# A key's and queries' rotary partner by transfers inside SBUF instead of products with constant matrices

## The reference, cut to what matters

```
q = rmsnorm(q.reshape(B, S, 8, 64), g_q);  k = rmsnorm(k.reshape(B, S, 2, 64), g_k)
q = apply_axial_rope(q, cos, sin);         k = apply_axial_rope(k, cos, sin)

def rotate_half(a):
    a1, a2 = jnp.split(a, 2, axis=-1)
    return jnp.concatenate([-a2, a1], axis=-1)

def apply_axial_rope(x, cos, sin):
    xr, xc = jnp.split(x, 2, axis=-1)
    rot = jnp.concatenate([rotate_half(xr), rotate_half(xc)], axis=-1)
    return x * cos + rot * sin
```

## Time and profile before

| | us |
|---|---|
| median of 3 runs | 750.63 |
| lowest and highest | 750.09, 750.79 |
| span of the profiled execution, first to last instruction | 747.1 |
| TensorE busy in it | 731.6 |
| VectorE busy | 585.6 |
| ScalarE busy | 467.6 |
| GpSimd busy | 147.4 |

### The profile page before, as it was taken

One profiled execution on the slowest core, in us unless ns is written; L12 is line 12 of the kernel. 1 busy time (PEld: TensorE's weight loads), 2 busy tenths in 40 slices (PEclk: granted clock), 3 DMA queues, 4 the chain that ended last, 5 costly groups with the idle time before them and its releaser, 6 DMA issues.

```text
span 747.1 us, 14444 instructions
## 1 busy us (share of the span) xinstructions
PE 731.6 (98%) x5355; PEld 670.1 (90%) x5355; DVE 585.6 (78%) x868; ACT 467.6 (63%) x789; POOL 147.4 (20%) x141
## 2 busy tenths in 40 slices
PE   8999999999999999999999999999999999999996
PEld 7899999888999798998889888997889999999995
DVE  7997989844976577786686998988789888866667
ACT  7878775659765475455554539668686555555565
POOL 5000000001234024333232330010003212343330
PEclk9999999999999999999999999999999999999999
DMA  8554444155555849889787882953237775566551
GB/s 303 162 179 148 157 135 130 48 140 186 173 180 177 309 148 405 302 299 329 240 267 275 265 323 78 347 189 99 82 109 228 259 236 187 183 193 192 179 170 57
DMA packets 47314, 150.68 MB, mean 202 GB/s; under 512 B 9472, under 2 KB 10888, under 8 KB 47256
## 3 DMA queue, kind: packets, MB, share of 16 engines
q1 hardware_dynamic: 45272, 145.86, 58.3%
q10 hardware_dynamic: 1984, 4.03, 1.6%
HBM read 147.73 MB, written 1.06 MB: 199 GB/s over the span
## 4 chain that ended last, share of the span: by engine, by line
PE 80%; DVE 9%; ACT 4%; issue 2%; SPq 2%; DMA 2%; ACTq 0%; DVEq 0%
PE ps L823 29%; PE ps L764 19%; PE ps L511 17%; DVE wl L1767 2%; PE ps L1066 2%; SPq L409 1%; ACT wh L1181 1%; PE ps L1126 1%; PE ps L618 1%; PE ps L1007 1%; DMA ada_w<-in_w_ada 1%; PE ps L637 1%; PE ps L525 1%; PE ps L529 1%; PE ps L526 1%
## 5 line engine op out<-in xcount | busy, mean ns | idle before, releaser
L1767 DVE TENSOR_TENSOR wl<-raw,wh 128x1024 fp32r<-128x1024 f32 x220 | 283.6, 1295 | 88.2 <-ACT wh L1181 86.6
L1181 ACT ACTIVATE wh<-raw 128x1024 fp32r<-128x1024 f32 x220 | 231.5, 1055 | 70.2 <-PE ps L764 46.5
L823 PE MATMUL ps<-xh,wh 128*128 128x256 f32 x672 | 189.7, 282 | 0.5 <-ACT zv L1630 0.5
L823 PE MATMUL ps<-xh,wl 128*128 128x256 f32 x672 | 188.2, 280 | 0.0
L823 PE MATMUL ps<-xl,wh 128*128 128x256 f32 x672 | 188.1, 280 | 0.0
L823 PEld LDWEIGHTS ps<-xh,wh 128*128 128x128 f32 x672 | 126.5, 188 | 4.9 <-issue 2.1
L823 PEld LDWEIGHTS ps<-xl,wh 128*128 128x128 f32 x672 | 126.5, 188 | 1.9
L823 PEld LDWEIGHTS ps<-xh,wl 128*128 128x128 f32 x672 | 126.7, 189 | 0.0
L511 PE MATMUL ps<-xh,wh 128*128 128x256 f32 (+2 forms) x400 | 116.8, 292 | 1.3 <-DVE wl L1767 0.6
L511 PE MATMUL ps<-xh,wl 128*128 128x256 f32 (+2 forms) x400 | 113.2, 283 | 0.0
L511 PE MATMUL ps<-xl,wh 128*128 128x256 f32 (+2 forms) x400 | 113.1, 283 | 0.0
(11 more groups left out here) (420 smaller groups left out, 1238.0 us busy)
## 6 DMA issues: line engine op xcount, KB each, us to landing
raw<-in_w_stream SPq DMA_DIRECT2D x220, 512.0 KB, 4.1
ada_w<-in_w_ada SPq DMA_DIRECT2D x48, 512.0 KB, 6.3
vtk<-in_x SPq DMA_DIRECT2D x2, 512.0 KB, 4.7
tg_m<-in_ln_rows ACTq DMA_DIRECT2D x2, 512.0 KB, 6.7
out<-ob SPq DMA_DIRECT2D x4, 256.0 KB, 2.0
u<-uT SPq DMA_DIRECT2D x16, 34.0 KB, 2.6
eepp<-in_s_mats SPq DMA_DIRECT2D x1, 512.0 KB
decay_rows<-decay_dram SPq DMA_DIRECT2D x4, 128.0 KB
```

The costliest lines, as they stand in the source:

```text
L823: mm = nc.tensor.matmul(ps[:, bank, 0:SEQ], w, x, start=(k == 0), stop=(k == 3 * KD - 1))
L1181: nc.scalar.activation(wh[:, b % RING], raw[:, b % RING], ACT.Identity).then_inc(hi_done, 1)
L1767: V.tensor_tensor(wl[:, b % RING], raw[:, b % RING], wh[:, b % RING].bitcast(F32), ALU.subtract).then_inc(lo_done, 1)
```

## The change

The head dimensions of q and k are put in another order by the host (columns of the weights, the gains): 0 to 15, 32 to 47, 16 to 31, 48 to 63. The partner of a dimension then lies 32 partitions away, for both axes at once, and the sign goes into the sine table. In place of `turn_pairs`, ScalarE's queue issues four DMAs for each tile that exchange neighbouring groups of 32 partitions of `qg` into `qrot` (now with two buffers). In place of `swap_k` it issues two DMAs that exchange the halves of the finished key. VectorE multiplies the fetched partner in SBUF by the sine. The constant matrices go, bank 3 keeps v alone, and VectorE's `q_finish(2)` moves behind `maxima(1)`.

```diff
-            def turn_pairs(t):
-
-                bank3(lambda: nc.tensor.matmul(ps[:, 3, 0:SEQ], cst[:, C_ROT:C_ROT + P], qg[:, t % 3, :], start=True, stop=True))
 
             def k_stat():
 
                 pe.wait_ge(S["q_ev"], 1)
                 nc.tensor.matmul(ps[:, 2, 0:SEQ], cst[:, C_BLK:C_BLK + P], qs[:, 0, :], start=True, stop=True).then_inc(S["q_stat"], 1)
-                turn_pairs(0)
...
-                turn_pairs(i + 1)
-
-            def swap_k():
-
-                pe.wait_ge(S["qk_ready"], 1)
-                bank3(lambda: nc.tensor.matmul(ps[:, 3, 0:SEQ], cst[:, C_SWAP:C_SWAP + P], kf[:, 0, :], start=True, stop=True))
...
                 pe.wait_ge(S["qk_ready"], 2 + i)
                 if i == 0:
-                    pe.wait_ge(S["b3_free"], 4)
+                    pe.wait_ge(S["respread"], 544)
                     pe.wait_ge(S["tok_pre"], QT)
...
                 if n == 12:
-                    swap_k()
                     tok_ms()
...
+            def fetch_partner(t):
+
+                act.wait_ge(S["q_ev"], t + 1)
+                if t >= 2:
+                    act.wait_ge(S["qk_ready"], t - 1)
+                for a in range(0, P, HD // 2):
+                    z = a + HD // 2 if a % HD == 0 else a - HD // 2
+                    act.dma_start(qrot[z:z + HD // 2, t % 2, :], qg[a:a + HD // 2, t % 3, :]).then_inc(partner(t)[0], 16)
+
+            def swap_k():
+
+                act.wait_ge(S["qk_ready"], 1)
+                for n in range(2):
+                    act.dma_start(kf[HD * (1 - n):HD * (2 - n), 1, :], kf[HD * n:HD * (n + 1), 0, :]).then_inc(S["respread"], 16)
+
...
                     if t >= 3:
                         act.wait_ge(S["qk_ready"], t - 2)
                         act.wait_ge(S["q_stat"], t - 2)
-                        act.wait_ge(S["b3_full"], ROTATED[t - 3])
                     nc.scalar.activation(qs[:, t % 3, :], p_, ACT.Square)
                     nc.scalar.activation(qg[:, t % 3, :], p_, ACT.Identity, scale=col("g_q" if t else "g_k"))\
                         .then_inc(S["q_ev"], 1)
+                    fetch_partner(t)
+                    if t == 2:
+                        swap_k()
...
             def q_finish(t):
 
                 dst = qf[:, t - 1, :] if t else kf[:, 0, :]
-                dve.wait_ge(S["b3_full"], reads[0] + 1)
+                dve.wait_ge(S["q_ev"], t + 1)
                 if t == 0:
                     dve.wait_ge(S["mixing_landed"], 48)
-                bank3_read(V.tensor_tensor(qrot[:, :], ps[:, 3, 0:SEQ], rope[:, 1, :], ALU.mult))
                 step(V.tensor_tensor(dst, qg[:, t % 3, :], rope[:, 0, :], ALU.mult))
-                dve.wait_ge(S["b3_free"], reads[0])
-                ins = V.tensor_tensor(dst, dst, qrot[:, :], ALU.add)
+                dve.wait_ge(*partner(t))
+                step(V.tensor_tensor(qrot[:, t % 2, :], qrot[:, t % 2, :], rope[:, 1, :], ALU.mult))
+                ins = V.tensor_tensor(dst, dst, qrot[:, t % 2, :], ALU.add)
...
                 if n == 12:
                     q_finish(1)
-                    dve.wait_ge(S["b3_full"], reads[0] + 1)
-                    bank3_read(V.tensor_copy(kf[:, 1, :], ps[:, 3, 0:SEQ]))
                 if n == 13:
-                    q_finish(2)
                     q_scales(0)
                     maxima(0)
                     maxima(1)
+                    q_finish(2)
                 lo(B_IN2 + n + AHEAD)
```

More of the change, by code:

```diff
@@ L87 @@
 NGATE = 32 + HEADS
-C_ID, C_ONE, C_BLK, C_ROT, C_SWAP, C_MASK, C_T = 0, 128, 256, 384, 512, 640, 768
+C_ID, C_ONE, C_BLK, C_MASK, C_T = 0, 128, 256, 384, 512
 C_ONE_ = C_T + NCK
@@ L265, in two_blocks @@
         qstd = sb("qstd", [P, 2, SEQ])
-        qrot = sb("qrot", [P, SEQ])
+        qrot = sb("qrot", [P, 2, SEQ])
         qf = sb("qf", [P, QT, SEQ])
@@ L314, in two_blocks @@
             "z_act", "zv_turned", "zv_copied", "zv_ms", "zv_std", "zv_n", "mixed", "tok_pre", "tok_done", "tok_sq", "tok_pairs", "tok_sum",
-            "q_ev", "q_stat", "q_std", "b3_full", "b3_free", "v2_ev", "qk_ready",
+            "q_ev", "q_stat", "q_std", "even_partner", "odd_partner", "v2_ev", "qk_ready",
             "s_done", "max_done", "exp_done", "pt_done", "pt_copied", "o_done", "ao_done", "ao_turned",
@@ L364, in lo_made, with partner @@
             return lo_done, t + b + 1
+        def partner(t):
+            return S["odd_partner" if t % 2 else "even_partner"], 64 * (t // 2 + 1)
         def turned_at(tag, m):
@@ L905, in mix_tokens @@
                 mm.then_inc(S["mixed"], 1)
[L907 to L914, removed]
             def turn_v2():
@@ L919, in turn_v2 @@
                 pe.wait_ge(S["zv_copied"], NT)
[L921 to L925, removed]
-            def turn_pairs(t):
-                bank3(lambda: nc.tensor.matmul(ps[:, 3, 0:SEQ], cst[:, C_ROT:C_ROT + P], qg[:, t % 3, :], start=True, stop=True))
+                for c in range(NT):
+                    mm = nc.tensor.transpose(ps[:, 3, c * P:(c + 1) * P], vv[:, c * P:(c + 1) * P], ident)
+                mm.then_inc(S["zv_turned"], 1)
             def k_stat():
@@ L996, in weigh_v @@
                 if i == 0:
+                    pe.wait_ge(S["zv_n"], NT + 1)
                     pe.wait_ge(S["q_std"], 3)
                     pe.wait_ge(S["branch_std"], NT)
-                elif i == 1:
-                    pe.wait_ge(S["b3_free"], 7)
-                else:
+                elif i >= 2:
                     pe.wait_ge(S["branch_lo"], QT + i - 1)
@@ L2370, in _ @@
                     dve.wait_ge(S["mixing_landed"], 48)
-                    dve.wait_ge(S["b3_full"], reads[0] + 1)
-                    bank3_read(V.tensor_copy(vtok[:, :, :].rearrange("p s e -> p (s e)"), ps[:, 3, 0:SEQ]))
+                    dve.wait_ge(S["zv_turned"], NT + 1)
+                    V.tensor_copy(vtok[:, :, :].rearrange("p s e -> p (s e)"), ps[:, 3, 0:SEQ]).then_inc(S["zv_n"], 1)
                     for m in range(QT):
@@ L2655 @@
     up2, down2 = _tiles(w2), I["w_down_2"][0].reshape(KF2, P, D)
-    t2 = _tiles(w1)
+    pairs = np.concatenate([np.arange(0, 16), np.arange(32, 48), np.arange(16, 32), np.arange(48, 64)])
+    heads = np.arange(5 * P).reshape(-1, HD)[:, pairs].reshape(-1)
+    t2 = _tiles(np.concatenate([w1[:, heads], w1[:, 5 * P:]], 1))
     att, tok = I["w_out_2"][0].reshape(2, D // 2, D)
@@ L2692 @@
         "b_ada": _cols(I["b_ada_2"][0].reshape(NMOD, D)[list(MOD_ORDER)].reshape(-1)), "g_norm1": _cols(I["g_norm1_2"][0]),
-        "g_q": twice(I["g_q_2"][0]), "g_k": twice(I["g_k_2"][0]), "g_tok_v": twice(I["g_tok_v_2"][0]),
+        "g_q": twice(I["g_q_2"][0][pairs]), "g_k": twice(I["g_k_2"][0][pairs]), "g_tok_v": twice(I["g_tok_v_2"][0]),
         "g_attn": _cols(I["g_attn_out_2"][0]), "g_tok": _cols(I["g_tok_out_2"][0]), "g_norm2": _cols(I["g_norm2_2"][0]),
@@ L2708 @@
         consts[64 * g:64 * g + 64, C_BLK + 64 * g:C_BLK + 64 * g + 64] = 1.0 / HD
-    for o in range(P):
-        a = o % 32
-        src, sign = (o + 16, -1.0) if a < 16 else (o - 16, 1.0)
-        consts[src, C_ROT + o] = sign
-        consts[(o + 64) % P, C_SWAP + o] = 1.0
     consts[:, C_MASK:C_MASK + P] = np.where(np.arange(P)[:, None] <= np.arange(P)[None, :], 0.0, -1e30)
@@ L2719 @@
     ar, ac = ((n // 64).astype(f)[:, None] * inv, (n % 64).astype(f)[:, None] * inv)
-    ang = np.concatenate([ar, ar, ac, ac], 1).T
-    rope = np.stack([np.concatenate([np.cos(ang)] * 2), np.concatenate([np.sin(ang)] * 2)], 1).astype(f)
+    ang = np.concatenate([ar, ac], 1).T
+    rope = np.stack([np.concatenate([np.cos(ang)] * 4), np.concatenate([-np.sin(ang), np.sin(ang)] * 2)], 1).astype(f)
     arrays = {
```

6 lines of the change are left out of this document (removed).

## The result

| | before | after |
|---|---|---|
| median, us | 750.65 | 760.17 |
| lowest and highest, us | 750.09, 750.79 (4 runs) | 758.60, 761.45 (4 runs) |
| span of the profiled execution, us | 747.1 | 756.8 |
| TensorE busy in it, us | 731.6 | 731.4 |

The change makes the kernel slower: the ratio is 1.0132, with a 95% interval of 1.0119 to 1.0144. The forecast was 756.0 us and its range ended at 759.6, so the sign was right and the size was not. The profile after is that of the fastest of the four executions (758.60 us); the medians are compared, and the profile is read for where the time goes.

What follows compares the result with a forecast made beforehand. TensorE was taken as the bound, with ScalarE and VectorE equally late at two points. Its 2.6 us saved go into waiting, and ScalarE's issues make the stage 5.4 us late: 750.6 + 5.4 = 756.0 us, range 750.1 to 759.6.

Steps and rivals of the forecast that it cites:

- What is added on ScalarE: 22 DMA issues in ScalarE's instruction stream, 0.38 us each from start to start, delaying everything of ScalarE's behind them.
- 760 at 0.63: Forecast time in us if each issue takes 0.63 us, with ScalarE's fourth fetch overtaking VectorE by 0.6 us.
- dear issues: Rival: issues cost 0.60 us, as transfers inside SBUF on SyncE; 760 us, range 757.5 to 761, chance 0.12.
- Step 1: After tile 1's evacuation: four issues put the weights' high part at 496.8, key ready at 500.45 instead of 498.98.
- Step 2: Tile 2's fetches and the swap: six issues, 2.3 us, over at 502.8; scores of pair 0 stand until 504.7.
- Step 3: Query statistics' root at 508.7, first exponentials at 510.6, scores of pair 1 at 513.3, 4.3 us late.
- Step 4: VectorE's maxima and rotations set the exponentials of heads 2 and 3 at 517.1, 5.4 us late.
- Step 5: From those exponentials through the weighting of v to the kernel's end, everything simply starts 5.4 us late.
- Cheap issues: Rival: issues cost ScalarE next to nothing and VectorE sets the stage's end; 750.2 us, no change, chance 0.13.
- The clock: Rival: TensorE's clock falls in its stands, 4.0 us at 509.3 being the border; 757.5 to 759.5 us, chance 0.10.
- Faster: Rival: fetches end before holding anyone, so TensorE's 2.6 us come through; 748.0 us, chance 0.09.
- Late landing: Rival: transfers land late, ahead of scores of pair 0; up to 3 us beyond 2.2 stays hidden, changing nothing.

Runs made afterwards that it cites:

- prices: Kernel after plus eight groups of four DMA issues on ScalarE's queue behind the last store; issues with both ends in SBUF took 0.51 to 0.62 us each.
- sp_swap_early: Against sp_queue, the key's swap is issued one weight block earlier in SyncE's order; 750.05 us, ratio 1.0004 to the kernel before.
- keep_clock: Kernel after with 28 idle constant products on TensorE ahead of the scores of pair 0; 758.95 us, ratio 1.0127 to before.
- sp_maxima_first: Against sp_swap_early, VectorE's rotation of pair 2 moved behind the maxima of heads 2 and 3; 748.18 us, ratio 0.9978 to before.
- swap_first: Kernel after with the two swap issues ahead of the third fetch, all still on ScalarE's queue; 759.27 us, ratio 1.0129 to before.
- sp_queue: Kernel after with all 22 transfers on SyncE's queue and the swap ahead of the fetch for tile 2; 753.45 us, ratio 1.0051 to before.
- hbm_source: Kernel after with every fetch and swap reading a constant HBM table instead of the SBUF tiles; 757.16 us, ratio 1.0104 to before.

## Why the prediction was right and wrong

**The step that failed is the term "What is added on ScalarE"**, the price of an issue: 0.38 us taken, with 0.33 and 0.63 as ends; 0.61 measured, some 0.64 from start to start. The row of the transfer inside SBUF, 0.60, was on the table and was called the nearest in bytes and partitions; it was then put aside because its pattern has more dimensions. The plain rectangles took 0.61 all the same, and the prices run shows that with both ends in SBUF neither bytes nor rows count. At 0.25 more for each of 14 issues in a row that is 3.5 us, and the prediction's own line for it, "760 at 0.63", is what came: 760.17. The profile agrees: its span is 9.7 us longer, where that line makes it 9.5. That the median hits the line within 0.2 us is partly luck. The prediction carried over the 3.5 us between span and median as fixed; in the profiled execution of the kernel after 1.8 us lie outside the span, and the median is 1.6 above that execution for a reason that wasn't seen. The chance of 0.12 on dear issues was too small, and the range ended 0.6 us under the measured time, though the text had priced this case at up to 761.

**Step 1** (high part at 496.8, key ready at 500.45): 497.94 and 501.7. The fetch adds 2.68 us between evacuation and high part (3.04, from 494.90 to 497.94, against 0.36) instead of 1.67.

**Step 2** (six issues over at 502.8, scores of pair 0 at 504.7): 505.6 and 507.99. The six issues took 3.8 us instead of 2.3, on top of the late key. What I left out of the prediction is TensorE's stand of 1.70 us at 499.50: `q_stat(0)` waits for ScalarE's root of the key. It cost nothing of its own, since TensorE would have stood that much longer ahead of the scores.

**Step 3** (root 508.7, first exponentials 510.6, scores of pair 1 at 513.3): 512.54, 514.40 and 517.12, so 3.8 us beyond, of which 3.5 are the price and 0.17 the stage's later start. That the exponentials wait for ScalarE's own stream and no longer for VectorE's maxima is as said: the 0.94 us of idling ahead of them is gone.

**Step 4** (517.1 for the exponentials of heads 2 and 3, by VectorE): 521.42, by ScalarE. VectorE's 7.7 us from its first maximum were right (513.26 + 7.7 = 520.96), and the fourth fetch overtakes it by 0.46 us, where the text had 0.6 for a price of 0.63.

**Step 5** (one constant shift from there): right in form. 9.74 us at the exponentials, 9.87 at the weighting of v, 9.7 in the span. "The 2.6 us taken from TensorE are spent in waiting" is right too, and sp_swap_early shows that they would have been spent so even with free issues.

**The rivals.** Cheap issues: refuted at once, no issue was under 0.51. The Trainium skill (SBUF — State Buffer, "The DMA setup-cost knee") gives the setup two parts, some 50 ns of the sequencer and a few hundred ns of descriptor generation; the prediction took only the first for what ScalarE loses. The 0.61 us measured here is nearer to both together. As a thought experiment the case was well priced: with the issues off ScalarE's stream sp_swap_early came out at 1.0004, where the text had 750.2, and its exponentials of head 2 are 0.34 us early, where the text had 0.4. Dear issues: this is what happened. The clock: it did fall, to 0.50 within the stand of 4.18 us. The Trainium skill (TensorE: Matmul & The Clock Gate, "What's actually happening") says that the slow state is the default and that activity lifts it; the trace agrees, with 0.50 from 506 on, after TensorE's last matmul at 503.8. The prediction's border at a stand of 4 us does not hold: the clock fell 2.2 us into this one, and stands of 2.53 and 2.54 us went either way (last section). keep_clock shows that the fall lay beneath ScalarE's delay and did not add to it. Faster: the gain exists, and it took a queue that nobody waits behind, an earlier swap and a new order on VectorE. That its 748.0 was near the 748.18 of sp_maxima_first is luck, since the path was another: it is VectorE's order behind the exponentials of pair 0 and not their start that decided. Late landing: the swap took 3.1 us to land instead of 2.2, and swap_first and keep_clock move the scores of pair 0 by -3.2 and +2.4 us with the stage within 0.2 us of that of the kernel after, so this slack is real while ScalarE is as late as there. In sp_queue it is gone, and the landing is what is left.

## What to carry to other kernels

Count what a DMA issue costs the engine that issues it, by a row of the trace whose two ends lie in the same kinds of memory, and put the issues on a queue behind which nothing urgent stands; then look at what that queue itself waits for ahead of them. Work taken from the busiest engine pays only up to the next engine's order: where two engines arrive at a point within a few tenths of a microsecond, the order of the second may have to be changed with it; here each of the two edits alone measured as nothing.

## What the runs showed of the hardware

An issue with both ends in SBUF held the engine for 0.61 us, on ScalarE (kernel after, prices) as on SyncE (sp_queue: a group of four in 2.44 to 2.52 us), and on ScalarE for 8 KB as for 128 KB. In prices 32 rows from HBM took 0.44 and a row to HBM 0.27; other shapes with an end in HBM took 0.33 to 0.61. Single issues took longer: 1.47 us in the first fetch of the kernel after (a group of four in 3.40 us instead of 2.44), 1.93 in hbm_source; why is open. Twenty-eight small constant products in two passes took 6.50 us, 0.12 for a pass, so such filling must be counted in full where something waits behind it.

The length of a stand alone did not decide over TensorE's clock. In keep_clock it stayed at 2.4 GHz through a stand of 2.54 us (scores of pair 1, 1.13 us long), in hbm_source it fell to 1.2 GHz within one of 2.53:

```profile
523.39 2.08 PE L956 MATMUL ps<-kf,qf 64*128 64x256 f32 x8 [2.53 <-DVE qf L2302]
```

In swap_first it fell 1.4 us after TensorE had taken up work again behind a stand of only 0.94 us (506.43, mean clock 0.92 in 507 to 508), and in sp_queue 0.7 us after one of 3.35. What else decides is open here.
